# Hybrid decoder step on one core: router on summed, unnormalised rows inside the last projection, bf16 counts, a shorter way to the first one-hot, and gamma and beta of the last norm loaded late

## The chip, the cores and the metric

The kernel runs on one core of a Trainium2 chip. The metric is the device time of one execution in microseconds (us); before the change the median of 3 runs was 1156.62 us (1155.09 to 1158.95).

## The reference, cut to what matters

One decoder layer for a prompt of 256 tokens and for 8 samples, which share the weights. D is 1024; there are 32 experts, of which each token takes 4. Everything is float32 at the interface.

```python
proj = x @ w_in                                    # pool input, q, k, v, o, gates
mix  = concat([pool_out, h]) @ w_out               # h: matrix-memory heads, normalised and gated
x1   = layer_norm(DN_ALPHA * x + mix, ln1_g, ln1_b)
logits = x1 @ w_router + b_router
top_v, top_e = top_k(logits, 4);  gates = softmax(top_v)
# per expert e, over the tokens that chose it:
h = xb @ w1[e] + b1[e];  glu = min(h[:, ::2], 7);  lin = clip(h[:, 1::2], -7, 7)
ff += gate * ((glu * sigmoid(1.702 * glu) * (lin + 1)) @ w2[e] + b2[e])
x2 = layer_norm(DN_ALPHA * x1 + ff, ln2_g, ln2_b)
y  = x2 + sigmoid(x2 @ w_ple_gate) * (p @ w_ple)
```

The states of pool and memory are outputs too. The weights of the experts are 32 x 12 MiB and are all read.

## The kernel before

Each engine has one program written out by hand; semaphores order them. The 264 tokens are three chunks: 0 and 1 of 128 prompt tokens, 2 of the 8 samples. The router works in the order 0, 2, 1 (`ORDER`).

**Stages.** TensorE transposes x, makes 20 tiles of the input projection (`project(t)`, L494) with the memory's products between them, and then the output projection (`mix`, L667). Chunk 0 gets all eight k-slices of w_out into banks 0 and 1, chunk 1 into banks 2 and 5; the samples go through L735 (four column blocks to partitions 0, 32, 64 and 96 of one bank). `mix_ps` counts finished pieces.

**First norm.** VectorE adds the residual out of PSUM (`residual`, L1237), takes statistics (`half_stats`, `moments`), and makes scale and shift from the root that ScalarE returns (`ln1_scale`). ScalarE normalises the rows in `xtok` (`ln1_rows`, L1590), without gamma and beta, which go into the router's weights (GpSimd, L1776; the bias row on TensorE, L601 and L602) and into the experts' operand later.

**Router.** TensorE transposes the normalised rows (`turn_x1`, L681; `turn_samples`, L689), ScalarE copies them to `x1T` (L1598), TensorE multiplies them as stationary operand with the weighted router (`router`, L697 and L699), and VectorE's `route` takes the best four, a one-hot of them and their sum, `mask`; then, after ScalarE's exp, the gates. TensorE counts places per expert with float32 products of the masks (`count_places`, L751 to L756, bank 3). VectorE turns the counts into `pos_table` for all five passes (L1289, L1291), and `one_hot(0, 0)` (L1298, L1300) makes the selection of expert 0.

**Loop.** For each expert `gather` (L771) collects its tokens with the one-hot, TensorE transposes them (L806), VectorE applies gamma and beta (`turned`), TensorE adds bias (L819) and multiplies with w_mlp1 (L831) and w_mlp2 (L870), and `combine` (L793, L799) and VectorE's `accumulate` (L1326, L1331) add the result of the expert before to `total`. `total` starts as ALPHA times the normalised rows with gamma and beta (`begin_sum`, L1381 and L1382).

**Weights.** They go through a ring of 16 slots of 1 MiB, 12 slots per expert, all from SyncE's queue (L378). Units 0 to 11 are loaded while the earlier stages run. Units 12 to 15 wait for `mix_ps` 5, since w_out lies in their slots. Unit n from 16 on waits for `units_used` n - 15, which TensorE raises after the last matmul that reads a slot.

**End.** After the loop the second norm, the embedding and its gate follow. `affine` (L1431, L1432) applies the second gamma and beta from `lnreg`, where GpSimd's queue has loaded them (L1813 to L1818) once `total` is started and the first norm's rows there are read.

`step(ins)` on VectorE raises a semaphore with the instruction and waits for it; `more(ins)` only raises it.

## Time and profile before

| | before |
|---|---|
| median of 3 runs | 1156.62 us |
| profiled execution, its own time | 1157.18 us |
| its span, first to last instruction | 1155.2 us |
| mean TensorE clock | 0.986 of full |
| busy share: TensorE, VectorE, ScalarE, GpSimd | 97%, 35%, 14%, 7% |
| DMA, mean over the span | 381 GB/s, 439.93 MB |
| packets under 512 B | 12527 of 74161 |
| chain that ended last | TensorE 73%, DMA 10%, VectorE 7%, SyncE's queue 6% |

The shares are of the whole span, most of which is the expert loop. A busy share of 97% doesn't say that TensorE is the bound, since its clock and its waits for operands are inside it; the stages have different limits and are read one by one. Clock is in shares of 2.4 GHz (0.50 is 1.2 GHz). In a row of the timeline the first number is the start, the second the length of a group of instructions, and in brackets stands the idle time before it with what ended it.

### The profile page before, as it was taken

The numbers are of one execution on the slowest core, as the hardware profiler recorded it, in microseconds if no ns is written. First come the engines' busy times: TensorE is split into PE (matmuls) and PEld (weight loads), VectorE is DVE, ScalarE is ACT, GpSimd is POOL, SyncE is SP. The second block draws the span as 40 slices with busy tenths as digits, with TensorE's granted clock in tenths as the row PEclk, the third lists the DMA queues.
The fourth block names the chain that finished last, engine by engine and source line by source line (L and its number), as shares of the span: only waits on it lengthen the run. The fifth ranks groups of instructions, "written<-read, shape, count | busy, mean of one in ns | idle before, by whom it ended". The sixth has DMA issues, their size and how long they took to land.

```text
span 1155.2 us, 15251 instructions
## 1 busy us (share of the span) xinstructions
PE 1124.9 (97%) x5726; PEld 438.1 (38%) x5726; DVE 399.8 (35%) x803; ACT 157.8 (14%) x274; POOL 76.0 (7%) x110
## 2 busy tenths in 40 slices
PE   8999989999999999999999999999999999999998
PEld 5887453333333333333333333333333333333344
DVE  1656564333333333333333333333333333333254
ACT  1522130000100010001000100010001000100042
POOL 0746411000000000000000000000000000000000
PEclk9999959999999999999999999999999999999999
DMA  9986758999999999999999999999999999999951
GB/s 317 289 333 241 218 202 319 421 421 421 422 421 422 422 422 422 422 422 422 422 422 422 422 422 422 422 422 422 422 422 422 422 422 422 422 422 422 421 200 38
DMA packets 74161, 439.93 MB, mean 381 GB/s; under 512 B 12527, under 2 KB 13803, under 8 KB 24626
## 3 DMA queue, kind: packets, MB, share of 16 engines
q1 hardware_dynamic: 72665, 435.37, 92.7%
q0 software_dynamic: 1184, 3.71, 0.9%
q10 hardware_dynamic: 288, 0.56, 0.1%
q8 instruction: 13, 0.21, 0.1%
q14 instruction: 11, 0.08, 0.0%
HBM read 436.07 MB, written 3.77 MB: 381 GB/s over the span
## 4 chain that ended last, share of the span: by engine, by line
PE 73%; DMA 10%; DVE 7%; SPq 6%; issue 2%; ACT 2%; DVEq 0%
PE bank L831 33%; PE bank L870 16%; DMA ring<-in_w_mlp 9%; PE bank L494 6%; SPq L378 5%; PE bank L793 5%; PE bank L954 2%; DVE proj L1358 2%; PE bank L667 2%; DVE proj L1355 2%; PE bank L856 2%; ACT wpool L1635 1%; DVE proj L1352 1%; DVE proj L1350 1%; PE bank L819 1%
## 5 line engine op out<-in xcount | busy, mean ns | idle before, releaser
L831 PE MATMUL bank<-ring,proj 128*64 128x512 f32 x2048 | 470.1, 599 | 3.1 <-DMA ring<-in_w_mlp 3.1
L831 PEld LDWEIGHTS bank<-ring,proj 128*64 128x64 f32 x2048 | 135.7, 136 | 290.3 <-issue 251.1
L870 PE MATMUL bank<-ring,wpool 128*64 128x512 f32 x1024 | 226.8, 595 | 8.2 <-ACT wpool L1635 8.2
L1326 DVE SCALAR_TENSOR_TENSOR xT<-bank,proj,xT 128x512 f32<-128x512 f32 x128 | 90.2, 747 | 391.6 <-PE bank L793 391.6
L870 PEld LDWEIGHTS bank<-ring,wpool 128*64 128x64 f32 x1024 | 71.3, 137 | 143.1 <-issue 131.7
L771 PE MATMUL bank<-xreg,proj 128*64 128x512 f32 (+1 forms) x396 | 98.1, 613 | 1.8 <-DVE sel L1300 1.8
L1630 ACT ACTIVATE proj<-proj 128x512 f32<-128x512 f32 x32 | 20.2, 632 | 552.4 <-DVE proj L1350 552.4
L793 PE MATMUL bank<-mixT 64*128 64x512 f32 x264 | 75.3, 647 | 0.9 <-ACT mixT L1638 0.9
L1350 DVE TENSOR_SCALAR proj<-bank 128x256 f32<-128x256 f32 x64 | 24.2, 420 | 150.0 <-PE bank L831 150.0
L494 PE MATMUL bank<-xT,ring 128*128 128x264 f32 x320 | 75.4, 394 | 0.7 <-DMA ring<-in_w_in 0.7
L494 PEld LDWEIGHTS bank<-xT,ring 128*128 128x128 f32 x320 | 61.4, 194 | 12.5 <-issue 1.9
L771 PEld LDWEIGHTS bank<-xreg,proj 128*64 128x64 f32 (+1 forms) x396 | 25.6, 137 | 67.3 <-issue 65.4
L1638 ACT COPY mixT<-bank 128x512 f32<-128x512 f32 x32 | 18.7, 585 | 230.5 <-PE bank L870 230.5
L1331 DVE SCALAR_TENSOR_TENSOR hist_mix<-bank,proj,hist_mix 128x128 f32<-128x128 f32 x66 | 20.1, 346 | 70.2 <-PE bank L799 70.2
L793 PEld LDWEIGHTS bank<-mixT 64*128 64x128 f32 x264 | 20.1, 186 | 54.7 <-issue 54.7
L1358 DVE TENSOR_TENSOR proj<-proj 128x512 f32<-128x512 f32 x32 | 33.8, 1056 | 1.1
L1316 DVE TENSOR_TENSOR proj<-bank,small 128x512 f32<-128x512 f32 x33 | 22.8, 692 | 28.2 <-PE bank L806 28.2
L954 PE MATMUL bank<-ring,mixT 128*128 128x512 f32 (+1 forms) x80 | 28.2, 509 | 0.2 <-issue 0.2
L667 PE MATMUL bank<-ring,mixT 128*128 128x512 f32 x64 | 28.2, 595 | 0.1
L1633 ACT COPY hist_mix<-bank 128x512 f32<-128x512 f32 x32 | 18.7, 585 | 41.6 <-PE bank L771 41.6
L1352 DVE TENSOR_SCALAR proj<-bank 128x256 f32<-128x256 f32 x64 | 23.9, 415 | 0.0
L1319 DVE TENSOR_TENSOR proj<-proj,small 128x512 f32<-128x512 f32 x33 | 22.9, 693 | 1.1
(324 smaller groups left out, 654.6 us busy)
## 6 DMA issues: line engine op xcount, KB each, us to landing
ring<-in_w_mlp SPq DMA_DIRECT2D x384, 1024.0 KB, 24.9
ring<-in_w_in SPq DMA_DIRECT2D x10, 1024.0 KB, 11.9
ring<-in_w_out SPq DMA_DIRECT2D x4, 1024.0 KB, 8.6
ring<-in_w_ple_gate SPq DMA_DIRECT2D x4, 1024.0 KB, 19.4
xreg<-in_x_prompt SPq DMA_DIRECT2D x4, 512.0 KB, 4.7
ring<-q_row SPq DMA_DIRECT2D x1, 2048.0 KB, 7.7
ring<-k_row SPq DMA_DIRECT2D x1, 2048.0 KB, 7.2
out<-ring POOLq DMA_DIRECT2D x1, 2048.0 KB, 16.7
```

Of the source, the lines that this page charges most:

```text
L378: sp.dma_start(unit_place(s, u), unit_weights(e, u)).then_inc(sem(f"slot{s}"), 16)
L494: last = pe.matmul(bank[t % 2][:, 0:TOK], w[:, k % 4, j * P:(j + 1) * P], xT[:, k, :], start=(k == 0), stop=(k == KD - 1))
L667: last = pe.matmul(banks[half][0:n, :], mixT[:, k, t0:t0 + n], w[:, k % 2, half * 512:half * 512 + 512], start=(k == 0), stop=(k == KD - 1))
L771: last = pe.matmul(bank[2][BLOCK * h:BLOCK * (h + 1), :], onehot[0:m, c, 0:BLOCK], xtok[0:m, c, 512 * h:512 * h + 512], start=(c == 0), st ...
L793: last = pe.matmul(banks[h][:, :], hotT[half, buffer, c * P:(c + 1) * P], eout[half, :], start=True, stop=True)
L831: last = pe.matmul(bank[q][BLOCK * t:BLOCK * (t + 1), :], xgT[:, k % 4, k // 4, :], ring[:, s, col:col + 512], start=False, stop=(k == KD ...
L870: last = pe.matmul(bank[4][BLOCK * h:BLOCK * (h + 1), :], aT[:, m, BLOCK * t:BLOCK * (t + 1)], w[:, k % 2, 512 * h:512 * h + 512], start=F ...
L954: last = pe.matmul(GATE_BANKS[c][i], x2T[:, k, t0:t0 + n], gate_weights(k)[:, PIECES[c][i]], start=(k == 0), stop=(k == KD - 1))
L1326: ins = STT(total[:, c, s], ins_bank[h][:, :], gate_table[:, c, bass.ds(n, 1)], total[:, c, s], ALU.mult, ALU.add)
L1350: TS(glu[:, q, :], hb[q][:, 0, :], LIMIT, None, ALU.min).then_inc(sem("glu_ready"), 1)
L1352: TS(lin[:, q, :], hb[q][:, 1, :], LIMIT, -LIMIT, ALU.min, ALU.max).then_inc(sem("lin_ready"), 1)
L1358: TT(act_out.rearrange("p (q a x) -> p q x a", q=2, a=2), lin.rearrange("p q (x a) -> p q x a", a=2), sig.rearrange("p q (x a) -> p q x a" ...
```

## The change

- **Order.** TensorE transposes the rows as soon as alpha * x + mix is summed (`rows_summed`), not when they are normalised. It does so for chunk 0 before the second half of chunk 1's projection, which is cut in three parts; the routers of chunks 0 and 2 stand between them.
- **Algebra.** For a row s with scale r and shift -m * r, logits = r * (s @ (gamma * W)) + (-m * r) * colsum(gamma * W) + (beta * W summed + b). `row_terms` holds the two sums for all partitions. TensorE makes it from sums of VectorE in the place of the old bias row; ScalarE copies it, and TensorE waits for that copy (`terms_done`) before it overwrites the bank.
- **Router.** The weights are the stationary operand (32 columns), the transposed rows move; k-slices k % 4 go to partitions 32 * (k % 4). ScalarE copies the four parts (`parts_out`), and `logit_rows` adds them with `stack4` and puts tokens on partitions.
- **Routing.** `route` only makes the mask. Negated maximum (`peak_of`), the exp, now of all 32 logits, and the sum over the mask (`gates_of`) come later; GpSimd makes a gate table with one operation per chunk instead of four.
- **Counts** are bf16, start from FAR, and go straight into the first pass's part of `pos_table`. The other passes' parts come after `passes_ready`.
- **Normalising** of a chunk now follows its transposes; gather waits for `ln1_ready` 6.
- **Last gamma and beta** (2 x 512 KB) move from GpSimd's queue at the loop's start to SyncE's, behind the gate weights.
- Some semaphores are merged, among them those of glu and lin inside the expert.

```diff
 # SyncE, behind the gate weights
+            for i, src in enumerate((ln2_g, ln2_b)):
+                sp.dma_start(lnreg[:, D * i:D * i + D], src.partition_broadcast(P).rearrange("p o d -> p (o d)"))\
+                  .then_inc(sem("ln2_in"), 16)
 # TensorE
-            for k in range(KD):
-                pe.matmul(bank[7][0:1, 0:EXPERTS], ln1_cols[:, 1, k:k + 1], wrout[:, k, :], start=(k == 0), stop=False)
-            pe.matmul(bank[7][0:1, 0:EXPERTS], ones[0:1, 0:1], brout[:, :], start=False, stop=True)\
-              .then_inc(sem("brow_ps"), 1)
...
+            pe.matmul(bank[7][:, 0:2 * EXPERTS], ones, row_terms, start=True, stop=False)
+            pe.matmul(bank[7][:, EXPERTS:2 * EXPERTS], ones[0:1, :], brout[:, :], start=False, stop=True)\
+              .then_inc(sem("wsum_ps"), 1)
             project(19)
-            pe.wait_ge(sem("pool_done"), 4)
+            pe.wait_ge(sem("terms_done"), 1)
...
+            def turn_rows(c, half, ready):
+
+                n = CHUNKS[c][1]
+                pe.wait_ge(sem("rows_summed"), ready)
+                b, at = TURNED[c][half]
+                for k in range(4 if c < 2 else KD):
+                    kk = 4 * half + k
+                    width = n if c == 2 else P
+                    last = pe.transpose(b[:, at + k * width:at + k * width + n],
+                                        xtok[0:n, c, kk * P:(kk + 1) * P], ident[0:n, 0:n])
                 last.then_inc(sem("x1T_ps"), 1)
 
             def router(c, done):
 
                 t0, n = CHUNKS[c]
                 pe.wait_ge(sem("x1T_done"), done)
-                pe.matmul(logits_bank[c][0:n, 0:EXPERTS], ones[0:1, 0:n], brout[:, :], start=True, stop=False)
                 for k in range(KD):
-                    last = pe.matmul(logits_bank[c][0:n, 0:EXPERTS], x1T[:, k, t0:t0 + n], wrout[:, k, :],
-                                     start=False, stop=(k == KD - 1))
-                last.then_inc(sem("logits_ps"), 1)
+                    q = k % 4
+                    last = pe.matmul(logits_bank[c][32 * q:32 * q + EXPERTS, 0:n], wrout[:, k, :], x1T[:, k, t0:t0 + n],
+                                     start=(k < 4), stop=(k >= 4))
+                last.then_inc(sem("part_ps"), 1)
+
+            def logit_rows(i):
+
+                c = ORDER[i]
+                n = CHUNKS[c][1]
+                pe.wait_ge(sem("part_done"), i + 1)
+                pe.matmul(logits_bank[c][0:n, P:P + EXPERTS], LOGIT_PARTS[c], stack4, start=True, stop=True)\
+                  .then_inc(sem("logits_ps"), 1)
...
-            mix(1, second, range(4, KD))
-            turn_x1(0, 0, 0)
-            turn_samples()
-            pe.wait_ge(sem("wr_ready"), 1)
+            turn_rows(0, 0, 1)
+            turn_rows(0, 1, 2)
+            mix(1, second, range(4, KD), (0,))
+            pe.wait_ge(sem("wsum_ready"), 2)
             router(0, 2)
-            turn_x1(1, 4, 1)
+            turn_rows(2, 0, 3)
+            logit_rows(0)
             router(2, 3)
+            mix(1, second, range(4, 6), (1,))
+            logit_rows(1)
+            mix(1, second, range(6, KD), (1,))
+            turn_rows(1, 0, 4)
+            turn_rows(1, 1, 5)
             router(1, 5)
...
+            pe.matmul(bank[3][:, 0:3 * EXPERTS], ones16[0:1, :], far_row, start=True, stop=False)
             count_places(0, (2, 1))
             count_places(2, (1,))
+            logit_rows(2)
             pe.wait_ge(sem("mask_ready"), 3)
             count_places(1, ()).then_inc(sem("pos_ps"), 1)
...
+            pe.wait_ge(sem("ln1_ready"), 6)
             pe.wait_ge(sem("onehot_ready"), 2)
             gather(0)
 # VectorE
+            step(dve.tensor_reduce(stack4, ident.rearrange("p (q e) -> p e q", q=4), AX.X, ALU.add))
+            dve.wait_ge(sem("wr_ready"), 1)
+            more(dve.tensor_reduce(row_terms[:, 0:EXPERTS], wrout[:, :, :].rearrange("p k e -> p e k"), AX.X, ALU.add),
+                 "wsum_ready")
+            more(dve.tensor_reduce(row_terms[:, EXPERTS:2 * EXPERTS], wbeta.rearrange("p k e -> p e k"), AX.X, ALU.add),
+                 "wsum_ready")
             dve.wait_ge(sem("tok_ps"), 3)
...
             residual(1, 0, bank[2])
+            route(0)
             ln1_scale(1, 2)
-            step(dve.memset(pos_table, FAR))
+            route(1)
+            peak_of(0)
+            peak_of(1)
             dve.wait_ge(sem("mix_ps"), 5)
             residual(1, 1, bank[5])
             moments(1, "row_mv")
+            more(dve.memset(combine_in, 0.0))
             ln1_scale(2, 1)
-            more(dve.memset(combine_in, 0.0))
-            more(dve.memset(sample_sum, 0.0))
-            route(0)
-            route(1)
             route(2)
 
             dve.wait_ge(sem("pos_ps"), 1)
 
-            step(STT(posm, mask, -FAR, bank[3][:, 0:3 * EXPERTS].rearrange("p (c e) -> p c e", c=3), ALU.mult, ALU.add))
+            first = pos_table[:, :, 0:EXPERTS]
+            step(STT(first, mask, -FAR, bank[3][:, 0:3 * EXPERTS].rearrange("p (c e) -> p c e", c=3), ALU.mult, ALU.add))
...
             hot_turned(0, 0)
+            for i in range(3):
+                gates_of(i)
             begin_sum(total[:, 0, :], 0, "total_ready")
 # ScalarE, the new order
+            turned_rows(0, 0, 1)
+            turned_rows(0, 1, 2)
+            ln1_rows(0, 0, 2)
+            parts_out(0)
             ln1_root(1, 2)
+            turned_rows(2, 0, 3)
+            parts_out(1)
+            ln1_rows(1, 2, 3)
+            turned_rows(1, 0, 4)
+            turned_rows(1, 1, 5)
             ln1_root(2, 1)
+            parts_out(2)
+            ln1_rows(2, 1, 5)
```

## Rows read from the trace of the kernel before

**Rows 1.** Table of stretches: busy us of each engine, clock, DMA share, GB/s.
```profile
core 0: us, PE busy (x) PEld busy (x) DVE busy (x) ACT busy (x) POOL busy (x), PEclk, DMA share, GB/s
160.00:177.00 17.00, 14.00 (x39) 4.75 (x41) 12.27 (x22) 4.47 (x9) 0.93 (x4) 0.50 0.00 0
...
178.00:182.00 4.00, 4.00 (x20) 1.34 (x20) 1.41 (x2) 0.00 (x0) 2.42 (x4) 1.00 0.78 303
...
210.00:890.00 680.00, 672.23 (x3470) 218.87 (x3468) 206.23 (x405) 64.40 (x101) 0.00 (x0) 1.00 1.01 422
```

**Rows 2.** Chain of waits in order of time: start, length, engine and line.
```profile
162.92 5.58 PE bank L771 x12
...
172.94 3.41 PE bank L831 x8
176.36 1.85 PE bank L793 x4
178.21 3.58 PE bank L831 x16
181.79 1.06 PE bank L793 x4
...
914.98 26.45 DMA ring<-in_w_mlp
```

**Rows 3.** Timeline, 70 to 92 us, TensorE and VectorE: start, length, operation.
```profile
71.68 0.63 PE L601 MATMUL bank<-wrout,small 128*1 128x32 f32 x16
...
88.19 0.69 DVE L1134 COPY xreg<-bank 128x512 f32<-128x512 f32 x1
...
91.81 1.05 PE L518 MATMUL bank<-xreg 128*128 128x128 f32 x8
```

**Rows 4.** Timeline of TensorE, 131 to 157 us.
```profile
132.60 3.64 PE L735 MATMUL bank<-ring,mixT 128*8 128x256 f32 x64 [1.09 <-DVE mixT L1212]
136.17 7.13 PE L667 MATMUL bank<-ring,mixT 128*128 128x512 f32 x16
143.14 1.04 PE L681 MATMUL bank<-cst,xreg 128*128 128x128 f32 x8
...
146.45 0.37 PE L697 MATMUL bank<-brout,cst 1*128 1x32 f32 x2 [0.53 <-ACT xT L1618]
...
153.40 3.62 PE L699 MATMUL bank<-wrout,xT 128*128 128x32 f32 x16
```

**Rows 5.** Timeline of VectorE, 132 to 179 us.
```profile
132.46 0.68 DVE L1237 SCALAR_TENSOR_TENSOR xreg<-xreg,bank 128x512 f32<-128x512 f32 x1
...
147.34 0.93 DVE L1281 MEMSET mixT<- 128x1040 f32 x1 [0.28 <-DVE stat L1231]
...
157.13 0.19 DVE L1245 COPY proj<-bank 128x32 f32<-128x32 f32 x1
...
158.47 0.37 DVE L1252 TENSOR_REDUCE proj<-proj 128x32 f32<-128x128 f32 x1
...
161.24 0.25 DVE L1289 SCALAR_TENSOR_TENSOR proj<-proj,bank 128x96 f32<-128x96 f32 x1 [1.75 <-PE bank L756]
...
162.65 0.22 DVE L1300 CAST sel<-cst 96x128 bf16<-96x128 f32 x1
...
165.28 1.21 DVE L1382 SCALAR_TENSOR_TENSOR proj<-lnreg,proj 8x1024 f32<-8x1024 f32 x1
...
178.44 1.41 DVE L1326 SCALAR_TENSOR_TENSOR xT<-bank,proj,xT 128x512 f32<-128x512 f32 x2 [1.30 <-PE bank L793]
```

**Rows 6.** Timeline of ScalarE, 137 to 152 us.
```profile
137.73 1.51 ACT L1612 COPY hist_mix<-bank 8x256 f32<-8x256 f32 x4
...
147.09 1.52 ACT L1590 ACTIVATE xreg<-xreg,stat 128x512 f32<-128x512 f32 x2 [0.48 <-DVE stat L1231]
...
151.79 0.58 ACT L1598 COPY xT<-bank 128x512 f32<-128x512 f32 x1 [0.27 <-PE bank L681]
```

**Rows 7.** Table of stretches as in rows 1: where the clock falls.
```profile
146.00:147.00 1.00, 0.55 (x4) 0.54 (x5) 0.32 (x2) 0.61 (x3) 0.00 (x0) 1.00 1.03 426
147.00:148.00 1.00, 1.00 (x8) 1.00 (x7) 0.72 (x2) 0.91 (x2) 0.00 (x0) 0.60 1.16 426
```

**Rows 8.** Line L450 in SyncE's queue: the gate weights from issue to landing.
```profile
L450 SPq DMA_DIRECT2D ring<-in_w_ple_gate x4: 677/3620/5723, 1084.3 to 1097.5; - x4
...
DMA to landing us min/median/max: 16.5/19.4/22.0
```

**Rows 9.** Timeline of VectorE, the tail, 1122 to 1146 us.
```profile
1122.02 1.21 DVE L1431 TENSOR_TENSOR xT<-xT,lnreg 128x1024 f32<-128x1024 f32 x1
...
1145.31 0.69 DVE L1440 TENSOR_TENSOR ring<-ring 128x512 f32<-128x512 f32 x1 [3.60 <-ACT ring L1694]
```

More of the change, by code:

```diff
@@ L659, in _, with mix @@
             last.then_inc(sem("cfin_ps"), 1)
-            def mix(c, banks, ks):
+            def mix(c, banks, ks, halves=(0, 1)):
                 t0, n = CHUNKS[c]
-                for half in range(2):
+                for half in halves:
                     for k in ks:
@@ L1024, in _ @@
             dve.wait_ge(sem("cst_in"), 16)
+            more(dve.tensor_copy(before16, cst[:, C_BEFORE:C_BEFORE + P]))
+            more(dve.tensor_copy(ones16, ones))
+            more(dve.memset(far_row, FAR))
+            more(dve.memset(mask, 0.0))
             dve.wait_ge(sem("gates_done"), 1)
@@ L1249, in route @@
+                step(dve.max(top[0:n, c, :], logits[0:n, c, :]))
+                step(dve.max_index(idx8[0:n, :], top[0:n, c, :], logits[0:n, c, :]))
                 step(dve.tensor_copy(idx4[0:n, :], idx8[0:n, 0:TOPK]))
-                step(TT(oh4[0:n, c], cst[0:n, C_EXP:C_EXP + EXPERTS].unsqueeze(1).to_broadcast([n, TOPK, EXPERTS]),
+                step(TT(oh4[0:n], cst[0:n, C_EXP:C_EXP + EXPERTS].unsqueeze(1).to_broadcast([n, TOPK, EXPERTS]),
                         idx4[0:n, :].unsqueeze(2).to_broadcast([n, TOPK, EXPERTS]), ALU.is_equal))
-                step(dve.tensor_reduce(mask[0:n, c, :], oh4[0:n, c].rearrange("p k e -> p e k"), AX.X, ALU.add),
-                     "mask_ready")
+                with nc.allow_low_precision(reason="a sum of zeros and at most one one"):
+                    step(dve.tensor_reduce(mask[0:n, c, :], oh4[0:n].rearrange("p k e -> p e k"), AX.X, ALU.add),
+                         "mask_ready")
@@ L1264, in _ @@
             moments(0, "row_mv")
-            step(dve.memset(mask, 0.0))
+            step(dve.memset(pos_table, FAR))
             ln1_scale(0, 0)
@@ L1370, in _ @@
             one_hot(0, 0)
-            step(TS(places, posm.unsqueeze(2).to_broadcast([P, 3, 2, EXPERTS]), FAR, None, ALU.add))
+            more(dve.tensor_copy(places, first.unsqueeze(2).to_broadcast([P, 3, 2, EXPERTS])))
+            peak_of(2)
             step(dve.tensor_reduce(gsum[:, 0:1], bank[3][:, 3 * EXPERTS:4 * EXPERTS], AX.X, ALU.max))
```

206 lines of the change are left out of this document (101 added, 105 removed).

## The prediction

> **What bounds the kernel now.** I read the table of stretches first. From 210 to 890 us the sixteen DMA engines are busy throughout and move 422 GB/s, at a TensorE clock of 1.00 [rows 1]. One expert's weights are 12 units of 1 MiB, 12.58 MB, so 29.8 us at that rate. The chain of waits names TensorE until 915 us and weight DMAs from there on [rows 2]: TensorE is slightly faster per expert, uses up the lead of the 16 ring slots, and then stands at the pace of the DMA. So the loop's end is the moment at which the stream of weights starts to run without a pause, plus the bytes that are left, over 422 GB/s. What is behind it (last expert, second layer norm, embedding) follows at a fixed distance.
>
> The stream starts when the first slot of expert 0 is freed, which L831's first eight instructions do: 172.94 + 3.41 = 176.35 us [rows 2]. From 160 to 177 us DMA moves nothing (0 GB/s) and TensorE has the lower of its two clock levels, 0.50, or 1.2 GHz [rows 1]. The DMA waits there for the router, so each microsecond by which 176.35 comes earlier should come off the end. The rest follows the router's path, and then asks what else touches the stream.
>
> **Part 1: the projections.** Sixteen router-bias instructions leave TensorE at 71.68 (0.63 us with their two companions left out) [rows 3]. Three matmuls that sum the gamma- and beta-weighted router come in before the last projection: about 0.45 us, by the 0.37 us of the one-row bias matmul [rows 4]. TensorE is full in this stretch, so that is -0.2 us. VectorE gets three reductions after the one that makes scq. The nearest is L1252, 0.38 us for 128 elements a partition [rows 5]; two of the new ones read 256, so 0.4 to 0.75 each and 1.2 to 1.9 together. The copy at 88.19 ends at 88.88 and TensorE reads its result at 91.81 [rows 3]: 2.9 us cover, 2.2 if TensorE runs 0.7 early. If the cover fell, TensorE would stall some 0.5 us. I take -0.2, bounds -0.6 to +0.5. The casts to bf16 at the start, GpSimd's second product and the small ScalarE copy are on engines that wait there; zero. TensorE's new wait for that copy (terms_done) stands before the ukeep transposes, behind a whole projection: zero.
>
> **Part 2: from the sample projection to the first gather.** Before, TensorE does L667 from 136.17 for 7.13 us, then transposes normalised rows at 143.14, waits for the samples, and runs three routers at the low clock; the last needs 3.62 us [rows 4]. After its mask, counting in f32 keeps VectorE idle for 1.75 us until 161.24; the one-hot is ready at 162.65 + 0.22 = 162.87, and gather starts at 162.92 [rows 2, 5].
> Now the new order on the same clock. Rows of chunk 0 are summed at 132.46 + 0.68 and 1.3 us later [rows 5], so the eight transposes start at 136.17 and take 0.9 (L681: 1.04 with its drain [rows 4]): 137.1. First half of L667's work, 3.5: 140.6. Meanwhile ScalarE copies the sample mix, 1.51 from 136.24, and the transposed rows, 2 x 0.58 [rows 6]: 138.9, in time. Router 0 is 16 instructions that write 32 partitions each, four groups side by side. The sample projection has that form: 64 in 3.64 us at 256 columns [rows 4], so 0.9 for 16: 141.5. Sample transposes 0.7, first logit matmul 0.4, router of the samples 0.7 (its operands come at 142.6 from ScalarE): 143.3. The second half of the projection in two pieces of 1.75 with one logit matmul between: 147.1, 4 us later than before.
> Then the last chunk's path: residual 0.7, which gives 147.8; four transposes 0.6, copy 0.6, router 0.9: 150.0. Copy of the parts 0.4; its logit matmul stands behind eight count matmuls of chunks 0 and 2 in TensorE's order, so 0.4 + 0.4: 151.4. Routing on VectorE from the read to the mask is 158.47 + 0.37 - 157.13 = 1.71 [rows 5], and with the gate arithmetic out of it 1.65: 153.0. Two bf16 counts and the wait 0.4; then only L1289's kind (0.25), the one-hot (0.35) and the cast (0.22), since the tables of later passes are made afterwards: 154.3. The memset of 0.93 [rows 5] is now between the last moments and the last scale; it delays nothing that is late, as the router is slower (logits 151.4, scale 150.3). ScalarE's last normalised rows, which gather now waits for, are ready at 150.4 + 1.52 [rows 6] = 151.9: zero.
> The clock: it was 1.00 until 147 and 0.60 in the next microsecond [rows 7], about 4 us after the last dense matmuls. Their end moves to 147.1, so I expect the fall near 151, and add 0.3 for what then runs at half rate. Gather starts at 154.6, or **8.3 us earlier**. Bounds: seven handoffs of TensorE, ScalarE and VectorE are new or moved, at up to 0.4 each above my steps (+3); with router matmuls hidden in loads 0.8 less.
>
> The Trainium skill (TensorEngine Tiling, Column Tiling) says that a stationary operand 32 columns wide allows four-fold column tiling, and that this mode excludes the f32 transpose mode. By the page alone the router's product would be a quarter of a serial one; the sum above goes by the sample projection's row, which agrees that groups overlap.
>
> **Part 3: from gather to the first freed slot.** 162.92 to 176.35 is 13.43 us, all at clock 0.50. The same instructions follow, so zero. VectorE ended the samples' begin_sum at 165.28 + 1.21, 3.6 us after the one-hot [rows 5]; with 0.15 for a peak and 1.1 for the memset and tables put before it, that is 154.3 + 4.9 = 159.2. It is needed when turn_places ends, 154.6 + 5.58 + 0.7 = 160.9: covered by 1.7 us, and late by the excess if gather gets quicker. Moved behind the first turned tile are six gate operations (product with sum, reciprocal, per chunk), at most 0.38 us each by L1252, so up to 2.3; I take 1.7. The first accumulate found VectorE idle 1.30 us [rows 5], so it comes 0.4 to 1.0 late. It ended at 179.85 and TensorE's next combine began at 181.79 [rows 2], so 1.9 us cover that; and slot 0 is free by then. Zero. (The gate table behind it, on GpSimd and ScalarE, has the 5 us of the two big begin_sums as cover.)
>
> **Part 4: gamma and beta of the last norm.** Two loads of 512 KB left GpSimd's queue at the loop's start and join SyncE's behind the gate weights. They are 1.05 MB / 422 GB/s = 2.5 us of stream. But the stream is not full there: 303 GB/s from 178 to 182 [rows 1]. If the hole only grows, the gain is 0; if it is all DMA time, 2.5. The second slot is freed 1.85 + 1.8 us after the first (a combine and half of L831's next 3.58 [rows 2]), against 2.5 per unit, so 1.1 of the place left may stay empty: 1.4. The two column loads, which stay, can fill it: 2.5. I take the middle, **-1.9**. At the end they land behind weights that take 16.5 to 22 us from issue (19.4 the median) [rows 8]. Issued near 1098, they come before 1120 + 2.5; VectorE multiplies by them at 1122.02 [rows 9]. If late by a microsecond or two, nothing moves: from 1122.02 to 1145.31, where the last chunk's output begins, VectorE has 23.3 us and is busy for 12.7 (eight full-row operations of 1.22, four half rows of 0.69, and gaps), so 10.6 us are spare.
>
> **Sum.** -0.2 - 8.3 - 0 - 1.9 = -10.4 us. The profiled execution took 1157.18 (span 1155.2), which gives 1146.8; the median of the three runs is 1156.62, 0.56 below it, which gives **1146.2**.
>
> **Rivals.**
> A: the clock comes back during gather. With gather dense for 5.58 us at 0.50 [rows 2], it could; against it, before had that very stretch and stayed at 0.50 for another 9 us. If it does half-way, gather gives 1.1, turn_places 0.35, the tile transposes and the bias matmuls 0.5 each, L831's first eight 1.7, less 0.4 for a late VectorE: 3.7 us, so 1142.5. The Trainium skill (TensorE: Matmul & The Clock Gate, HAM oscillation) says that sustained matmul work lifts the throttle and idle gaps bring it back. By it this rival is the rule; the row of 160 to 177 us speaks against it. I give it 20%.
> B: the handoffs. A chain through three engines with each step at its bound, and the clock down already before router 1, makes part 2 worth 5.0 instead of 8.3: 1149.5. For it: the old stretch has idle times of 0.5 to 1.8 us at such places. 18%.
> C: the change does not do what it says: logits wait for the row scales anyway, as the routing multiplies by them, and only the cheaper counts (1.3 us at the end of routing), the shorter one-hot path (0.8) and part 4 remain, 4.0 in all: 1152.6. Against it, scale 2 is ready before the last logits by my times. 3%.
> D, slower: the late rows of gamma and beta. They stall VectorE in front of 12.7 us of work. The end moves from the point where they land later than 1122.02 + 10.6 = 1132.6, and it eats the whole gain from 1143, 45 us after issue, where the slowest load of that stretch needs 22. At 50 us it would give about 1161. 2%.
>
> **How the numbers follow.** The forecast has 57%, its own range 1144 to 1149 (part 4 from 0 to 2.5, part 1, and a microsecond of handoffs). A range of 8 in 10 must take in B and most of A: 1141.5 to 1151.5. A measurement of this kernel can tell 0.3%, 3.5 us, from no change: below 1153.1 is faster. Forecast, A and B lie there, 0.95; C is at that border and counts as the same, 0.03; D is slower, 0.02.
>
> **What the profile after would show.** Right: gather's first matmul near 154.6, L831's first eight ending near 168.1; the idle stretch of DMA shorter, not gone, since units 12 to 15 are requested at 147 instead of 143 and need 10 us; 422 GB/s from some 180 on; the distance from the first freed slot to the end about 1.9 us shorter. Routers of chunks 0 and 2 at clock 1.00, between pieces of L667's work. Clock at 1.00 before 165 would be A; gather after 157 would be B; VectorE waiting for lnreg in the tail, D. I am wrong in the model itself if gather comes 8 us earlier and the end does not.

## The result, and the profile after

The changed kernel takes 1146.88 us (median of 4 runs, 1144.04 to 1147.71) against 1157.58 us of the kernel before beside it: a ratio of 0.9906, with a 95% interval of 0.9879 to 0.9932. It is 10.7 us faster (7.9 to 14.0 by that interval). In six more runs it took 1143.79 to 1147.16 us; the median of all ten is 1145.9.

The profiled execution took 1144.04 us, the lowest of its four; its span is 1142.3 us. First the table of stretches (us; busy time of each engine; then TensorE's clock, DMA share and GB/s), which answers [rows 1]:

```profile
150.00:157.00 7.00, 4.13 (x12) 1.26 (x14) 5.93 (x22) 2.96 (x6) 0.00 (x0) 0.52 1.02 430
157.00:160.00 3.00, 2.35 (x12) 0.76 (x10) 1.81 (x4) 0.59 (x1) 0.00 (x0) 0.99 0.22 90
160.00:164.00 4.00, 3.09 (x10) 1.13 (x12) 3.73 (x14) 0.00 (x0) 2.15 (x2) 0.57 0.00 0
164.00:170.00 6.00, 5.36 (x24) 1.36 (x20) 4.64 (x5) 3.89 (x8) 3.36 (x4) 1.00 0.65 221
170.00:178.00 8.00, 7.65 (x50) 2.37 (x52) 2.71 (x7) 0.00 (x0) 0.00 (x0) 1.00 1.00 339
210.00:890.00 680.00, 672.22 (x3460) 218.94 (x3456) 205.50 (x402) 64.93 (x102) 0.00 (x0) 1.00 1.01 422
```

The steady stretch is unchanged at 422 GB/s. What changed is ahead of it: DMA is idle for about 7 us (158 to 165) where it was idle for 17, and the clock, which stood at 0.50 from 148 to 177 before, comes back at 157 and for good at 164.

TensorE's timeline (start, length, engine, line, idle time before it) from the routers to the first gather; [rows 4] had this stretch before:

```profile
140.31 0.65 PE L698 MATMUL bank<-xT,wrout 128*32 128x128 f32 x16
141.85 0.31 PE L698 MATMUL bank<-xT,wrout 128*32 128x8 f32 x16
142.09 1.98 PE L675 MATMUL bank<-ring,mixT 128*128 128x512 f32 x4
144.16 1.98 PE L675 MATMUL bank<-ring,mixT 128*128 128x512 f32 x4
146.99 0.66 PE L688 MATMUL bank<-cst,xreg 128*128 128x128 f32 x4 [0.41 <-DVE xreg L1266]
148.32 0.65 PE L698 MATMUL bank<-xT,wrout 128*32 128x128 f32 x16 [0.68 <-ACT xT L1648]
149.41 0.41 PE L707 MATMUL bank<-cst,proj 128*128 128x32 f32 x2
151.70 0.21 PE L765 MATMUL bank<-mask,before 128*128 128x32 bf16 x1 [1.88 <-DVE mask L1283]
153.11 4.84 PE L787 MATMUL bank<-xreg,proj 128*64 128x512 f32 x12 [1.17 <-DVE sel L1340]
```

Gather starts at 153.11 instead of 162.92. The routers of chunks 0 and 2 (L698) lie between pieces of the projection (L675), and the last router takes 0.65 us instead of 3.62. Part of that is the clock, 1.00 here and 0.50 before; in f3 below, the same new router at 0.50 takes 1.08 us. Then the way into the loop, TensorE above and VectorE below:

```profile
161.76 2.95 PE L847 MATMUL bank<-ring,proj 128*64 128x512 f32 x8
164.64 1.13 PE L809 MATMUL bank<-mixT 64*128 64x512 f32 x4
165.70 3.65 PE L847 MATMUL bank<-ring,proj 128*64 128x512 f32 x16
170.35 1.13 PE L809 MATMUL bank<-mixT 64*128 64x512 f32 x4 [0.99 <-DVE xT L1366]
```
```profile
166.37 1.22 DVE L1428 SCALAR_TENSOR_TENSOR xT<-lnreg,xT 128x1024 f32<-128x1024 f32 x1
168.88 1.41 DVE L1366 SCALAR_TENSOR_TENSOR xT<-bank,proj,xT 128x512 f32<-128x512 f32 x2 [1.29 <-ACT hist_mix L1710]
```

The first eight L847 end at 164.7 instead of 176.4 [rows 2]; they free the first slot. But at the second combine (L809, 170.35) TensorE stands 0.99 us, for VectorE's first accumulate (L1366), which had itself waited 1.29 us. That wait is new, and it turned out to matter.

The late rows of gamma and beta are no trouble. SyncE's queue issues them here, and VectorE uses them at 1109.05:

```profile
1085.36 2.35 SPq L463 DMA_DIRECT2D lnreg<-in_ln_g  x1
1087.75 1.30 SPq L463 DMA_DIRECT2D lnreg<-in_ln_b  x1
```
```profile
1109.05 1.21 DVE L1479 TENSOR_TENSOR xT<-xT,lnreg 128x1024 f32<-128x1024 f32 x1
```

**Where the 12.9 us of span went.** I cut each trace at the start of the sample projection (S), the first gather, the first combine (C1, within 0.1 us of the moment the first slot is free) and the second combine (C2). Starts are TensorE's timeline; the medians of the other kernels are those of their own runs, the ratio is to the kernel before.

| kernel | median us | ratio, 95% | S | gather - S | C1 - S | C2 - S | end - C1 | end - C2 |
|---|---|---|---|---|---|---|---|---|
| before | 1157.58 | | 132.60 | 30.32 | 43.69 | 49.12 | 978.91 | 973.48 |
| after | 1146.88 | 0.9879-0.9932 | 132.28 | 20.83 | 32.36 | 38.07 | 977.66 | 971.95 |
| after, again | 1145.04 | 0.9879-0.9926 | 132.30 | 20.82 | 32.50 | 38.16 | 977.70 | 972.04 |
| e1 rows early | 1147.14 | 0.9889-0.9934 | 132.06 | 20.80 | 32.52 | 37.84 | 978.62 | 973.30 |
| e2 before, rows late | 1154.71 | 0.9959-0.9990 | 132.25 | 28.36 | 41.22 | 45.86 | 976.33 | 971.69 |
| e3 delay | 1152.82 | 0.9920-0.9968 | 134.22 | 25.63 | 39.00 | 44.48 | 977.98 | 972.50 |
| e4 filler | 1145.54 | 0.9873-0.9912 | 135.86 | 20.80 | 29.78 | 36.95 | 979.26 | 972.09 |
| f2 filler, gates | 1145.95 | 0.9878-0.9931 | 133.62 | 20.80 | 28.98 | 37.22 | 980.70 | 972.46 |
| f5 gates | 1146.76 | 0.9886-0.9930 | 134.19 | 20.79 | 32.51 | 38.61 | 978.30 | 972.20 |
| f3 unsplit | 1151.74 | 0.9927-0.9968 | 134.38 | 25.46 | 38.18 | 43.86 | 977.34 | 971.66 |
| f4 f32 counts | 1150.63 | 0.9913-0.9956 | 135.12 | 25.14 | 36.81 | 42.10 | 976.77 | 971.48 |
| f6 logit first | 1146.18 | 0.9884-0.9943 | 132.22 | 20.83 | 32.75 | 38.17 | 978.73 | 973.31 |
| g1 filler, GpSimd | 1149.21 | 0.9906-0.9957 | 135.15 | 24.52 | 35.83 | 40.48 | 976.42 | 971.77 |
| g2 GpSimd | 1149.15 | 0.9912-0.9957 | 132.33 | 24.50 | 36.02 | 40.66 | 976.95 | 972.31 |

Before to after: S -0.3, S to gather -9.5, gather to C1 -1.8, C1 to C2 +0.3, C2 to the end -1.5. That is 12.9. A row is one execution, and the same work does not always take the same time in it: e2's first difference from before lies behind the gather, and yet its gather comes 1.96 us sooner after S.

### The profile page after: what moved, and what is told of

It is laid out like the page before. It is cut to its first block, busy times and chain, and to the rows that moved or that the text cites. A ratio compares the mean times of both kernels' runs of the same rounds, so it can differ in the third digit from the quotient of the medians.

```text
span 1142.3 us, 15182 instructions
## 1 busy us (share of the span) xinstructions
PE 1110.4 (97%) x5704; PEld 427.0 (37%) x5704; DVE 400.9 (35%) x812; ACT 158.4 (14%) x277; POOL 75.2 (7%) x100
## 4 chain that ended last, share of the span: by engine, by line
PE 77%; DVE 9%; SPq 7%; DMA 3%; issue 2%; ACT 2%; DVEq 0%
PE bank L847 35%; PE bank L886 18%; PE bank L505 6%; SPq L387 6%; PE bank L809 5%; DVE proj L1397 3%; PE bank L971 2%; DMA ring<-in_w_mlp 2%; PE bank L675 2%; DVE proj L1394 2%; DVE proj L1392 2%; PE bank L872 2%; ACT wpool L1696 2%; DVE proj L1390 1%; PE bank L835 1%
## 5 line engine op out<-in xcount | busy, mean ns | idle before, releaser
L847 PE MATMUL bank<-ring,proj 128*64 128x512 f32 x2048 | 468.4, 598 | 2.5 <-DMA ring<-in_w_mlp 2.5
L847 PEld LDWEIGHTS bank<-ring,proj 128*64 128x64 f32 x2048 | 136.1, 137 | 287.7 <-issue 253.4
L1366 DVE SCALAR_TENSOR_TENSOR xT<-bank,proj,xT 128x512 f32<-128x512 f32 x128 | 90.2, 747 | 390.0 <-PE bank L809 388.7
L809 PE MATMUL bank<-mixT 64*128 64x512 f32 x264 | 74.5, 641 | 1.9 <-DVE xT L1366 1.0
L809 PEld LDWEIGHTS bank<-mixT 64*128 64x128 f32 x264 | 19.9, 184 | 55.1 <-issue 53.2
L675 PE MATMUL bank<-ring,mixT 128*128 128x512 f32 x64 | 28.7, 597 | 0.1
## 6 DMA issues: line engine op xcount, KB each, us to landing
out<-ring POOLq DMA_DIRECT2D x1, 2048.0 KB, 14.1
```

The lines of the kernel that those rows point to most:

```text
L675: last = pe.matmul(banks[half][0:n, :], mixT[:, k, t0:t0 + n], w[:, k % 2, half * 512:half * 512 + 512], start=(k == 0), stop=(k == KD - 1))
L809: last = pe.matmul(banks[h][:, :], hotT[half, buffer, c * P:(c + 1) * P], eout[half, :], start=True, stop=True)
L847: last = pe.matmul(bank[q][BLOCK * t:BLOCK * (t + 1), :], xgT[:, k % 4, k // 4, :], ring[:, s, col:col + 512], start=False, stop=(k == KD ...
L1366: ins = STT(total[:, c, s], ins_bank[h][:, :], gate_table[:, c, bass.ds(n, 1)], total[:, c, s], ALU.mult, ALU.add)
```

## Experiments

**The late rows, alone and undone.** e1 is after with the rows back on GpSimd's queue; e2 is before with only the rows late.

```diff
 # e1, from after (e2 is the reverse, from before)
-                sp.dma_start(lnreg[:, D * i:D * i + D], ...)      # SyncE, behind the gate weights
+                pool.dma_start(lnreg[:, D * i:D * i + D], ...)    # GpSimd, when total is started
```

> The changed kernel with one part undone: gamma and beta of the last norm are loaded from GpSimd's queue at the loop's start again. If those 1.05 MB take room in a full stream, the distance from the first freed slot (end of the loop's first eight matmuls, L847) to the end of the span grows by 1.9 us (1.4 to 2.5) over the changed kernel's 977.7; if the stream has a hole there anyway, it stays within 0.3 us. The time goes the same way: 1148.8 us against 1146.9.

> The kernel before with that one part of the change alone. The same theory gives a distance from the first freed slot to the end of 978.8 - 1.9 = 976.9 us and a time 1.9 us under the kernel before; the hole theory gives no difference; the rival that late rows hold up VectorE in the tail gives a longer distance. The first freed slot stays at 176.4 us in all of them.

Measured: e1 1147.14 us, where 1148.8 was expected, and its runs cannot tell it from after; e2 1154.71 us, ratio 0.9975 (0.9959 to 0.9990), so the part alone gives 1.2 to 4.7 us. The distance from C1 to the end, on which both expectations rest, grew by 1.0 us in e1 (1.4 to 2.5 expected) and fell by 2.6 in e2 (1.9 expected). From C2 it is a little steadier: with the rows early it is 973.48 and 973.30, with them late 971.48 to 973.31 in twelve traces, 972.1 in the mean. By that the part is worth about 1.3 us, half of the 2.5 us that its bytes take at 422 GB/s. This size is rough: there are only two traces with the rows early, and f6, with the rows late, lies with them at 973.31, for which I have no cause.

The expectation that e2's first slot would be free at 176.4 us was wrong, it was 173.5. Gather came sooner, in the very work that before does. TensorE in before, then in e2:

```profile
146.76 3.24 PE L699 MATMUL bank<-wrout,xT 128*128 128x32 f32 x16
149.81 1.95 PE L681 MATMUL bank<-cst,xreg 128*128 128x128 f32 x8
```
```profile
146.41 1.97 PE L702 MATMUL bank<-wrout,xT 128*128 128x32 f32 x16
148.22 1.24 PE L684 MATMUL bank<-cst,xreg 128*128 128x128 f32 x8
```

The clock is down from the microsecond at 147 in before (0.60 in it, then 0.50) and only from 149 in e2, and the first router and the transposes behind it are the 2.0 us. So S to gather in the old kernel is 28.4 or 30.3 us, and the 9.5 us between before and after are 7.5 by e2's trace.

**Gather late by a known amount.** e3 puts four memsets of `combine_in` on VectorE ahead of `first`.

```diff
             dve.wait_ge(sem("pos_ps"), 1)
+            for _ in range(4):
+                step(dve.memset(combine_in, 0.0))
             first = pos_table[:, :, 0:EXPERTS]
```

> The changed kernel with four more memsets of 0.93 us on VectorE just ahead of the first one-hot, 3.8 us in all. If the loop's end is the start of the weight stream plus a fixed distance, gather, the first freed slot and the end all move by 3.8 us: distance 977.7 (plus or minus 0.5), time 1150.7. If the loop took up part of a late start, the distance would shrink by some of the 3.8 us. The clock can blur it: where the clock rises at another place relative to gather, the step from gather to the first freed slot changes by up to 2 us, the distance behind it doesn't.

Measured: 1152.82 us, 5.9 more than after, where 3.8 was expected. Each memset takes 0.93 us and 0.28 to the next, 4.8 us in all; gather is 4.8 us later after S, C2 6.4 later, and the way from C1 to the end is the same within 0.3 us (977.98 against 977.66). So the loop takes up nothing of a late start. The other 1.6 us goes with the clock: in this trace it stayed at 0.50 from 155 to 174 us, through gather and to the first combine. (The traces themselves are 8.9 us apart; 1.9 of it lies before S, in a stretch of low clock that the last run of this section is about.)

**The clock.** e4 gives TensorE matmuls without use where it waits (2304 columns in five, into banks that are free).

```diff
             turn_rows(1, 1, 5)
+            filler(bank[5], 256)          # ident times 256 (512) columns of constants
             router(1, 5)
...
             logit_rows(2)
+            filler(bank[5])
+            filler(bank[5])
             pe.wait_ge(sem("mask_ready"), 3)
             count_places(1, ()).then_inc(sem("pos_ps"), 1)
+            filler(bank[5])
...
             spread_places(0)
+            filler(bank[2])
```

> The changed kernel plus five matmuls into banks that nobody reads, in the gaps of TensorE between the last router and the loop (one of 256 columns, four of 512). If low activity in those gaps is what brings the clock down, it stays at 1.00 and gather takes 2.9 us instead of 4.8: first freed slot 2.0 to 3.0 us earlier than 164.6 in the profile, and a median time of 1143 us, with less spread between executions (the changed kernel had 1144.0 to 1147.7). If the clock falls all the same, the fillers cost up to 0.5 us and the time is 1147.

Measured: the clock is 1.00 in each microsecond from 144 to 176, and C1 comes 29.78 us after S instead of 32.36. But C2 comes only 1.1 us sooner, as TensorE then waits 2.46 us for VectorE, and 1145.54 us is within the spread of after (1145.9 over ten runs); 1143 was expected. Its two shortest executions (1143.87 and 1143.97 us, at a mean clock of 0.999) are no shorter than after's (1143.79 to 1144.06, at 0.995 and 0.996). The Trainium skill (TensorE: Matmul & The Clock Gate, HAM oscillation) says that gaps in which TensorE waits bring the throttle back; with the gaps filled it did not come back in this stretch, so here the trace agrees. The same trace has two stretches of low clock, at 42 and at 107 us, in which TensorE had no such gaps (busy for 3.00 of 3 us from 42, 4.00 of 4 us from 106); the last section comes back to them.

**VectorE's order.** f2 is e4 with the gate sums ahead of the places and the samples' begin_sum behind hot_turned(0); f5 is the same move in after, without filler.

```diff
-            dve.wait_ge(sem("ln1_in"), 32)
-            begin_sum(sample_row, 2, "sample_begun")
+            for i in range(3):
+                gates_of(i)
             dve.wait_ge(sem("pos_ps"), 2)
...
             hot_turned(0, 0)
-            for i in range(3):
-                gates_of(i)
+            dve.wait_ge(sem("ln1_in"), 32)
+            begin_sum(sample_row, 2, "sample_begun")
```

> The kernel after with the five filler matmuls of the run before, and VectorE's three gate sums moved from behind hot_turned(0) to ahead of the places, with the first sum of the sample rows moved behind hot_turned(0) in their stead. Output unchanged. Theory: in the run with filler alone slot 0 was freed 8.98 us after the gather instead of 11.53, but the stream then took 916.61 us instead of 914.93, since TensorE waited 2.46 us at its second combine for VectorE's accumulate, which waited 1.30 us for ScalarE's copies of the sample sum, these being behind GpSimd's gate table. With the gates early, GpSimd's three instructions lie at 155 to 160 and ScalarE's copies end before VectorE's last total: VectorE's 1.3 us idle is gone, TensorE's wait falls to about 1.2 us, the stream takes 915 to 916 us: about 1 us less than with filler alone, 1144.5 us, 1.5 to 2.5 us under the kernel after. Rival: the stream is not limited by that wait (the ring refills from slots freed by TensorE either way), then the time is that of the filler alone, 1145.5 us. Second rival: the gate sums ahead of the places delay the turned rows by their 1.3 us, and everything is as far behind as it was ahead.

> The kernel after with only the moved gate sums and sample sum, without filler matmuls. Output unchanged. Theory: TensorE's 0.99 us wait at its second expert's combine (170.35) falls to nothing, and VectorE's gates fit into the 1.1 us in which it waited for the turned places, so slot 0 is freed no later: 0 to 1 us faster than the kernel after, 1146.4 us. Rival: VectorE's gates push the places back, slot 0 is freed up to 1 us later, 1147.9 us.

Measured: 1145.95 and 1146.76 us, no gain in either. TensorE's wait at C2, expected at about 1.2 us in f2 and at nothing in f5, is 3.53 and 0.72. In f2, TensorE and VectorE:

```profile
162.60 1.13 PE L818 MATMUL bank<-mixT 64*128 64x512 f32 x4
170.84 1.13 PE L818 MATMUL bank<-mixT 64*128 64x512 f32 x4 [3.53 <-DVE xT L1376]
```
```profile
166.85 1.22 DVE L1438 SCALAR_TENSOR_TENSOR xT<-lnreg,xT 128x1024 f32<-128x1024 f32 x1
169.38 1.41 DVE L1376 SCALAR_TENSOR_TENSOR xT<-bank,proj,xT 128x512 f32<-128x512 f32 x2 [1.30 <-issue]
```

Two things follow. The 1.3 us ahead of the first accumulate is not ScalarE's copies, as I had written for f2: they ended at 164.8 here, and the idle time is 1.30 us all the same. It is 1.29 in f5 too, where nothing that the profile shows ends it. That leaves VectorE's own way into the loop, its register load and branch; g1 tests it. And C1 is not what sets the end: in f2 it came 3.4 us sooner after S than in after, and the end only 0.3 (S to end: 1142.3 - 132.28 = 1010.0, and 1143.3 - 133.62 = 1009.7). While the stream still has holes (339 GB/s from 170 to 178), a stall of TensorE is a release that comes late; this reason is argued, no run tests it by itself. With the rows late, C1 to the end lies between 976.3 and 980.7 us, C2 to the end between 971.5 and 973.3.

**The projection not split.** f3 runs `mix(1)` whole before router(0).

```diff
-            mix(1, second, range(4, KD), (0,))
+            mix(1, second, range(4, KD))
             pe.wait_ge(sem("wsum_ready"), 2)
             router(0, 2)
...
-            mix(1, second, range(4, 6), (1,))
             logit_rows(1)
-            mix(1, second, range(6, KD), (1,))
             turn_rows(1, 0, 4)
```

> The kernel after with the second half of the prompt projection run whole ahead of router(0): TensorE's order is row turns, mix(1) both halves, router(0), sample turn, logit rows 0, router(2), logit rows 1, row turns, router(1). Output unchanged. It keeps the summed rows, the bf16 counts and the early one-hot, and takes away only that router and choice of two of three chunks lie inside the projection. Theory: the choice of chunks 0 and 2 (VectorE, some 1.7 us each) starts near 146 instead of 142 and now stands ahead of residual(1,1) in VectorE's order, so the last rows are turned 3 to 4 us later: the gather starts 3.3 us later, at 156.4, and the whole takes 1150 us. Rival: the summed rows alone give the gain, TensorE's work being the same in sum, and the gather moves by less than 1 us: 1147 us.

Measured: 1151.74 us. Gather is 4.6 us later (25.46 after S), where 3.3 was expected. TensorE in f3:

```profile
148.14 0.66 PE L688 MATMUL bank<-cst,xreg 128*128 128x128 f32 x4
152.52 1.11 PE L688 MATMUL bank<-cst,xreg 128*128 128x128 f32 x4 [3.73 <-DVE xreg L1264]
154.31 1.08 PE L698 MATMUL bank<-xT,wrout 128*32 128x128 f32 x16 [0.68 <-ACT xT L1646]
```

The last rows wait 3.73 us, because VectorE's choice for chunks 0 and 2 now stands ahead of the last residual. Less the 0.41 that they wait in after, that is the expected 3.3; of the rest, 0.9 is the clock, which falls in this wait (0.68 in the microsecond from 151, then 0.50), so that the transposes take 1.11 instead of 0.66 us and the last router 1.08 instead of 0.65. From gather to C1 another 1.2 us goes the same way.

**Counts in f32.** f4 keeps mask, far row and the two constant matrices in f32. The constants of the order matrix are taken from where `row_terms` lies in the kernel after, so the places that it counts are not the right ones; instructions, shapes and the totals per expert, hence the number of passes, are as in after.

```diff
-                pe.matmul(bank[3][:, a * EXPERTS:(a + 1) * EXPERTS], before16[0:m, :], mask[0:m, a, :],
+                pe.matmul(bank[3][:, a * EXPERTS:(a + 1) * EXPERTS], cst[0:m, C_BEFORE:C_BEFORE + P], mask[0:m, a, :],
...
-        mask = sb("mask", [P, 3, EXPERTS], BF16)[:, :, :]
+        mask = sb("mask", [P, 3, EXPERTS], F32)[:, :, :]
```

> The kernel after with the counts in f32: mask, the two constant matrices and the far row are f32, as the kernel before had them. Output unchanged. Theory (the prediction's step): the eight early count matmuls take about 1 us more ahead of logit rows 2, the two late ones 0.3 us more ahead of the first one-hot: the gather starts 1.3 us later and the time is 1148.2 us. Rival: the early ones lie in the time in which TensorE waits for ScalarE's logit parts (logit rows 2 start when the parts are copied, near 149.4), so only the late ones and the part beyond that count: gather 0.5 us later, 1147.4 us.

Measured: 1150.63 us, gather 4.3 us later; I had expected 1.3. Some of TensorE's rows in f4:

```profile
152.11 0.46 PE L773 MATMUL bank<-far_row,cst 1*128 1x96 f32 x2
152.50 0.41 PE L763 MATMUL bank<-mask,cst 128*128 128x32 f32 x2
152.74 1.00 PE L766 MATMUL bank<-mask,cst 128*128 128x32 f32 x4
154.10 0.63 PE L763 MATMUL bank<-mask,cst 8*128 8x32 f32 x2
154.55 0.61 PE L766 MATMUL bank<-mask,cst 8*128 8x32 f32 x2
155.51 0.64 PE L705 MATMUL bank<-cst,proj 128*128 128x32 f32 x2
158.03 0.64 PE L763 MATMUL bank<-mask,cst 128*128 128x32 f32 x2 [1.88 <-DVE mask L1279]
158.47 0.61 PE L768 MATMUL bank<-mask,cst 128*128 128x32 f32 x2
```

Far row to last logit matmul is 3.4 us (152.11 to 155.51) where after needs 0.5 (148.90 to 149.41), and the two late ones 1.05 instead of 0.24. An f32 product is two instructions here (x2) and a bf16 one is one. They stand on the path, since the logits of the last chunk are behind them in TensorE's order. Not all of the 3.4 us is the type: the clock falls to 0.50 just before 153, while they run. The product started at 152.50, at full clock, takes 0.24 us to the next start, those behind 154.10 take 0.42 to 0.54. At full clock throughout I would put the row of them at about 2.3 us (0.39 for the far row and eight times 0.24, an estimate).

**Last logits ahead of the counts.** f6 moves `logit_rows(2)` before the far row.

> The kernel after with the last logit matmul (logit rows 2) put ahead of the eight early bf16 count matmuls in TensorE's order. Output unchanged. Theory: the eight take about 0.5 us in which the copied logit parts may wait, and VectorE's choice of 1.9 us behind it covers them fully, so gather comes 0.1 to 0.5 us earlier and the time falls by as much: 1146.5 us. Rival: the counts already lie in the time that ScalarE needs for the parts (0.4 us), so nothing moves.

Measured: 1146.18 us, gather 20.83 us after S, as in after. The rival holds: the half microsecond of counts lies where TensorE waits for ScalarE's parts.

**VectorE relieved by GpSimd.** g1 is f2, g2 is f5, each with the samples' begin_sum as three GpSimd operations and VectorE's load of the number of passes ahead of its big sums.

```diff
 # GpSimd
             step(pool.memset(gate_table, 0.0))
+            pool.wait_ge(sem("mask_ready"), 3)
+            step(pool.tensor_tensor(sample_row, rows8, lnreg[0:SAMPLES, 0:D], ALU.mult))
+            step(pool.tensor_tensor(sample_row, sample_row, lnreg[0:SAMPLES, D:2 * D], ALU.add))
+            step(pool.tensor_scalar(sample_row, sample_row, ALPHA, None, ALU.mult))
```

> The kernel with filler matmuls and early gate sums, and in addition the samples' first sum made by GpSimd (two two-input operations and one with a constant, 8 rows of 1024) instead of VectorE, and VectorE's load of the number of passes ahead of its two big sums. Output unchanged. Theory: the end does not hang on the first freed slot but on the second combine, which in the runs so far stood 971.5 to 972.5 us ahead of the end whatever lay before it, while the first freed slot stood 976.3 to 980.7 ahead; with the clock held, that combine waits for VectorE (3.53 us). VectorE loses 2.4 us of work and up to 1 us of its 1.3 us ahead of the loop, so the second combine comes 34.8 us or less after the start of the sample projection instead of 37.2, its wait is about 1 us, and the time is 2 to 3 us below that of the filler kernels: 1143.3 us, 3.5 us below the kernel after. Rival: the first freed slot sets the end; it does not move, and the time stays at 1145.5 to 1146 us. Second rival: GpSimd beside VectorE slows both, the copies on ScalarE come late, and nothing is won.

> The same two changes on VectorE's side without filler matmuls. Output unchanged. Theory: TensorE's wait at the second combine (0.72 us in the run with early gates, 0.99 in the kernel after) goes away, the rest is TensorE at its lower clock: the second combine 37.3 us after the start of the sample projection instead of 38.1 to 38.6, and 1146.0 us. Rival: the wait moves to something else, 1146.9 us, as the kernel after.

Measured: 1149.21 and 1149.15 us, slower than after by 2.3 us against its first median and 4.1 to 4.2 against its second (1143.3 and 1146.0 had been expected); my theory fell, and the second rival came with a place that I had not seen. VectorE, then GpSimd, in g1:

```profile
155.32 1.92 DVE L1348 TENSOR_TENSOR proj<-cst,proj 128x192 f32<-128x192 f32 x1 [0.16 <-DVE proj L1343]
157.17 2.35 DVE L1350 CAST sel<-cst 96x128 bf16<-96x128 f32 x1
161.35 0.63 DVE L1430 TENSOR_TENSOR proj<-proj,cst 128x128 f32<-128x128 f32 x3
172.87 1.41 DVE L1376 SCALAR_TENSOR_TENSOR xT<-bank,proj,xT 128x512 f32<-128x512 f32 x2 [0.36 <-DVE xT L1438]
```
```profile
154.69 2.33 POOL L1879 TENSOR_TENSOR proj<-xreg,lnreg 8x1024 f32<-8x1024 f32 x1 [14.78 <-DVE mask L1293]
157.10 2.33 POOL L1880 TENSOR_TENSOR proj<-proj,lnreg 8x1024 f32<-8x1024 f32 x1
159.53 2.78 POOL L1881 TENSOR_SCALAR proj<-proj 8x1024 f32<-8x1024 f32 x1
```

The one-hot takes 1.92 us instead of 0.36 and the cast behind it 2.35 instead of 0.21; they end at 157.24 and 159.52, just behind a GpSimd operation each (157.02, 159.43). Gather is 3.7 us later, more than all that was to be won. The Trainium skill (SBUF — State Buffer, Who interferes with whom) describes this as an exclusive lock on shared ports, held for a whole instruction; the two pairs of rows agree. Not every pair does: GpSimd's third operation, a tensor_scalar, runs from 159.53 for 2.78 us, and within it VectorE's copy (159.44) and its three products of 128x128 with both operands in SBUF (161.35) take 0.34 and 0.63 us, as in after; of the small operations between them one takes 0.61 instead of 0.23. The last VectorE row is the half that worked: with the register load moved up, the idle time ahead of the first accumulate is 0.36 us instead of 1.30, and TensorE does not wait at C2 in g1 or g2 (C1 to C2 4.65 us). I did not run that half alone.

**After once more.**

> The kernel after itself once more, to see its spread beside the kernels above on the same chip. If the stretch of low clock at 40 to 46 us, which some kernels showed and the profiled execution of after did not, belongs to an execution and not to a kernel, this profile may show it, and then its sample projection starts 1.9 us later (134.2 instead of 132.3) and its time is near 1146 to 1147 us. If it is bound to a kernel, this one never shows it.

Measured: 1145.04 us (1143.79 to 1147.16, six runs), and its profiled execution (1144.39) is a twin of the first: S at 132.30, gather 20.82 after it. The stretch of low clock at 41 to 45 us does not show. Seven traces of other kernels have it, and in these S is 1.3 to 3.6 us late. This is e3, with work identical to after's until the last mask:

```profile
38.00:41.00 3.00, 2.99 (x18) 2.09 (x18) 1.12 (x5) 2.57 (x6) 2.68 (x5) 1.00 1.05 387
41.00:45.00 4.00, 4.00 (x9) 2.37 (x8) 2.16 (x8) 2.84 (x4) 3.30 (x10) 0.60 1.11 298
45.00:48.00 3.00, 3.00 (x14) 2.52 (x13) 0.41 (x2) 0.00 (x0) 2.68 (x5) 0.96 1.05 290
```

So the question stays half open. The work up to there is the same, and after's runs spread over 3.9 us, as such stretches would make them. The mean clock of each execution points the same way: after's four shortest (1143.8 to 1144.4 us) have 0.995 or 0.996, the six from 1145.7 to 1147.7 us have 0.991 to 0.994. But both traces of after are of executions near its lowest time, so where in its 1147 us the clock was low was never seen in a trace.

## Why the prediction was right

It said 1146.2 us in a range of 1141.5 to 1151.5; 1146.88 was measured (1145.9 over ten runs). Its sum was -10.4 us; the medians differ by 10.7, the two traces by 12.9.

- **The bound** held: 422 GB/s in the loop, and e3 shows that a late gather is a late end. The point from which the stream counts was only nearly right. It was named as the first freed slot; f2 moved that by 3.4 us and the end by 0.3. The second combine carries the end better, though not exactly (f6 is 1.3 us off).
- **Part 1**, -0.2 with the cover holding: S came 0.3 earlier. The three reductions took 0.39, 0.60 and 0.59 us, 1.6 in all against 1.2 to 1.9. The two new matmul groups took 0.7 us of TensorE (103.57 to 104.25) instead of 0.45.
- **Part 2**, -8.3: it was -9.5 against the trace that the prediction read, -7.5 against e2's trace of the same work. The order of events was as worked out, with each step a little sooner: logits at 149.8 (151.4 in the prediction, where its own terms add up to 151.2), mask at 151.65 (153.0), one-hot at 152.96 (154.3). The clock fell between 150 and 151 (0.62 in that microsecond), near the 151 that was said. Router 0 took 0.65 us instead of 0.9, that of the samples 0.31 instead of 0.7, and the last one 0.65 instead of 0.9. From mask to gather 1.6 was worked out and 1.5 measured. Rival B's dearer handoffs did not come (0.41, 0.68, 1.88 and 1.17 us idle at the four of the last chunk). The experiments say what the 9.5 stand on: without the split 4.6 are lost (f3), without bf16 4.3 (f4). They overlap, as both let the clock fall earlier, and are not to be added. No run takes away the summed rows, the router's new form or the short one-hot path alone, so their shares are not shown.
- **Part 3**, zero: C1 came 1.8 us sooner after gather, and C2 1.6. This is the step that was mis-sized. The clock came back at 157 to 160 and from 164, not in time for most of gather (4.84 us instead of 5.58) or the first eight (2.95 instead of 3.63 in the same view of before). By the prediction's own sign, a clock of 1.00 before 165, that is rival A, which had 20%, at half its size. The step "first accumulate late by 0.4 to 1.0, covered by 1.9 us" failed in its cover: the accumulate came 15.77 us after gather instead of 15.52, only 0.25 later in spite of the gate sums now ahead of it. But TensorE, at 1.00 for much of the way, was ready for the second combine 16.25 us after gather instead of 18.80. That uses up the 1.9 us and 0.9 more, the wait of 0.99. f5, with the gate sums elsewhere, still has 0.72 of it. Rival A's term of 0.4 for "a late VectorE" was the right idea at less than half its size, and e4 and f2 show why the rest of A would have given little: with the clock at 1.00 throughout, C2 comes 1.1 and 0.9 us sooner than in after, since VectorE's chain of places, turned tile, two big sums and loop entry ends hardly sooner.
- **Part 4**, -1.9 (1.4 by the gaps between freed slots): 1.3 by the mean distance, 1.5 in this pair, 1.8 from before to e2, each within the spread of the distances. Rival D had no part: the rows landed 15.2 and 15.8 us after their issue, and VectorE used them at 1109.05, 23.7 us after the first was issued, with no idle time ahead of it.
- **Rival C** had no part: routing waited 0.37 us for the last logit product, not for the row scales.

That the forecast met the median so closely is in part luck. In the pair of traces parts 2 and 3 gave 2.8 us more than was said, and 12.9 us is nearer to rival A's 14.1 than to the forecast's 10.4. The medians hide that for two reasons: the profiled execution of after was the lowest of its run, that of before near its median; and up to 2.0 us of part 2 is the early fall of the clock in the one trace of before that the prediction had.

## What to carry to other kernels

The first release need not be the start of a stream: check it by moving it alone, and look for a later one that comes late while the stream still has holes. Before taking one trace's stretch as the price of its work, look whether the clock stands the same in a second one: the old router cost 28.4 or 30.3 us. Before moving a product behind or ahead of a hand-off, count its instructions in the type that it will have: an order that costs half a microsecond in bf16 cost 3.4 in f32, some 1.1 of them, by the estimate above, through the clock that fell meanwhile. And before giving an idle GpSimd work with two operands in SBUF, see which VectorE operation on the critical path it will lie beside.

## What was not expected of the hardware

- A VectorE operation of 0.21 us took 2.35 us beside a GpSimd one of 2.33 us, and ended with it. Beside another GpSimd operation, a tensor_scalar, all but one of VectorE's took their usual time. In the kernel after, GpSimd's three gate tables take 3.79 us beside VectorE's sums, and 2.23 in f2 and g1.
- A loop entry with its register load costs VectorE 1.3 us of idle time, 0.36 when the load stands some operations earlier.
- The clock in the stretch after the router differs between kernels that differ little: low from 148 to beyond 176 in before, low from 149 to 172 in e2, which is the same work up to the gather, twice low and twice back in after. An estimate of a stretch like this should carry both levels.
- In seven traces the clock fell to 0.50 for about 3 us between 40 and 47 us although TensorE was busy throughout (4.00 of 4 us in e3's row above); in e4 once more at 106 to 110 us (0.58). The projections there (48 instructions) took 12.4 to 12.6 us instead of 10.95.
